# A float32 encoder trunk: VectorE's runs split, and the forget gate turned by VectorE and ScalarE in place of TensorE

## The reference, cut to what matters

```
def swiglu(h, w_in, w_out):
    a, b = jnp.split(h @ w_in, 2, axis=-1)
    return (jax.nn.silu(a) * b) @ w_out

# the recurrence of layer 1
proj = h @ w_in
q, f_pre, v, g_out = jnp.split(proj, 4, axis=-1)
f = lower_bound + (1.0 - lower_bound) * jax.nn.sigmoid(f_pre)
log_f = jnp.log(f); k = 1.0 - f
# per head of 128 features: scores from q, k and the running sum of log_f, then
# o = scores @ v, normalised, times silu(g_out), @ w_out

# the modulation, six vectors a layer, that scale, shift and gate both branches
mod = silu(c) @ w_ada[layer] + b_ada[layer]
```

## Time and profile before

| | us |
|---|---|
| median of 3 runs | 2146.22 (2145.55 to 2146.92) |
| the profiled execution, its own time | 2145.66 |
| its span, first to last instruction | 2143.9 |
| TensorE busy | 2086.6 (97% of the span) |
| VectorE busy | 1573.3 (73%) |
| ScalarE busy | 1142.7 (53%) |
| mean granted clock of TensorE | 0.989 of full speed |

### The profile page before, as it was taken

One profiled execution on the slowest core, in us unless ns is written; L12 is line 12 of the kernel. 1 busy time (PEld: TensorE's weight loads), 2 busy tenths in 40 slices (PEclk: granted clock), 3 DMA queues, 4 the chain that ended last, 5 costly groups with the idle time before them and its releaser, 6 DMA issues.

```text
span 2143.9 us, 25007 instructions
## 1 busy us (share of the span) xinstructions
PE 2086.6 (97%) x9575; PEld 1673.6 (78%) x9575; DVE 1573.3 (73%) x1617; ACT 1142.7 (53%) x1446; POOL 25.6 (1%) x95
## 2 busy tenths in 40 slices
PE   6879999999999999999999999999999999999998
PEld 2437888877788888788888888878888888888886
DVE  1248998889999887789897887677756676557645
ACT  2415544676665443465555565544456877654443
POOL 2000000000000000020000000000000000000000
PEclk7999999999999999999999999999999999999999
DMA  9999987788899898667676664678855666668664
GB/s 398 417 418 377 369 308 266 273 296 281 286 364 352 328 338 299 225 253 246 236 254 210 234 223 149 190 268 312 287 184 183 204 187 200 193 196 299 233 215 146
DMA packets 149594, 573.33 MB, mean 267 GB/s; under 512 B 17169, under 2 KB 17361, under 8 KB 141921
## 3 DMA queue, kind: packets, MB, share of 16 engines
q1 hardware_dynamic: 149474, 571.73, 75.3%
HBM read 569.56 MB, written 2.10 MB: 267 GB/s over the span
## 4 chain that ended last, share of the span: by engine, by line
PE 87%; DVE 5%; DMA 3%; ACT 3%; issue 2%; SPq 0%; DVEq 0%; ACTq 0%
PE prod L694 27%; PE prod L698 27%; PE prod L695 27%; PE modp L735 2%; DVE w_lo L1477 1%; ACT part_value L1264 1%; DMA ada_head<-in_ada_sections 1%; DMA ada_head<-in_ada_mixed 1%; DMA ada<-in_ada_sections 1%; DVE acc L1518 1%; ACT w_hi L1072 1%; PE small L986 1%; PE small L961 0%; PE small L794 0%; PE prod L668 0%
## 5 line engine op out<-in xcount | busy, mean ns | idle before, releaser
L1072 ACT ACTIVATE w_hi<-raw 128x1024 fp32r<-128x1024 f32 x696 | 735.3, 1060 | 791.7 <-PE prod L698 708.0
L1477 DVE TENSOR_TENSOR w_lo<-raw,w_hi 128x1024 fp32r<-128x1024 f32 x696 | 846.9, 1221 | 404.3 <-ACT w_hi L1072 400.7
L694 PE MATMUL prod<-w_hi,h_hi 128*128 128x512 f32 x2072 | 816.6, 394 | 9.0 <-DVE w_lo L1477 7.2
L695 PE MATMUL prod<-w_lo,h_hi 128*128 128x512 f32 x2072 | 807.7, 390 | 0.0
L698 PE MATMUL prod<-w_hi,h_lo 128*128 128x512 f32 x2072 | 807.7, 390 | 0.0
L694 PEld LDWEIGHTS prod<-w_hi,h_hi 128*128 128x128 f32 x2072 | 389.7, 188 | 97.6 <-DVE w_lo L1477 7.8
L698 PEld LDWEIGHTS prod<-w_hi,h_lo 128*128 128x128 f32 x2072 | 389.5, 188 | 82.0 <-DVE h_lo L1630 0.3
L695 PEld LDWEIGHTS prod<-w_lo,h_hi 128*128 128x128 f32 x2072 | 389.7, 188 | 78.7 <-issue 0.5
L1518 DVE SCALAR_TENSOR_TENSOR acc<-ada,cond,acc 128x1024 f32<-128x1024 f32 x255 | 325.8, 1278 | 1.9 <-DMA ada<-in_ada_sections 0.9
L694 PE MATMUL prod<-w_hi,g_hi 128*128 128x512 f32 x680 | 265.6, 391 | 0.0
L698 PE MATMUL prod<-w_hi,g_lo 128*128 128x512 f32 x680 | 264.6, 389 | 0.0
(11 more groups left out here) (217 smaller groups left out, 1030.3 us busy)
## 6 DMA issues: line engine op xcount, KB each, us to landing
raw<-in_w_ffn_in SPq DMA_DIRECT2D x352, 512.0 KB, 4.5
ada<-in_ada_sections SPq DMA_DIRECT2D x256, 512.0 KB, 6.0
raw<-in_w_ffn_out SPq DMA_DIRECT2D x176, 512.0 KB, 4.5
raw<-in_hgrn_w_in SPq DMA_DIRECT2D x128, 512.0 KB, 3.6
ada_head<-in_ada_sections SPq DMA_DIRECT2D x36, 1024.0 KB, 16.4
raw<-in_hgrn_w_out SPq DMA_DIRECT2D x32, 512.0 KB, 3.5
ada<-in_ada_sections SPq DMA_DIRECT2D x12, 1024.0 KB, 18.5
ada<-in_ada_mixed SPq DMA_DIRECT2D x16, 512.0 KB, 8.1
```

The source lines that it names most:

```text
L694: pe.matmul(o, hi[:, k, ts], wh, start=(begin and s == 0), stop=False)
L695: pe.matmul(o, hi[:, k, ts], wl, start=False, stop=False)
L1072: act.activation(w_hi[:, slot], raw[:, r], ACT.Copy).then_inc(hi_ready, 1)
L1477: dve.tensor_tensor(w_lo[:, slot], raw[:, r], w_hi[:, slot], ALU.subtract).then_inc(lo_ready, 1)
```

## The change

It has four parts.

1. **FFN blocks, VectorE** (both layers). The multiplication moves from step 4 to step 5 (`multiply_value`) and the turn from step 4 to step 7, so that one `w_lo` stands between the multiplication and the turn. ScalarE's sixteen copies begin one step later (`MOVE` 2).
2. **The forget values** of the recurrence. TensorE's eight transposes go. At step 22 of VectorE's list it turns the squares of `tok` into `feat` (`turn_forget`), ScalarE places them by sixteen plain copies to `fT` (`move_forget`, two a step from step 25 to 32), and one sigmoid of 128x1024 in place follows at step 34.
3. **Folds.** The unit (1, SC_F, 0) has its folds in steps 14 to 54 of the recurrence (before 16 to 80), (1, G_M, 1) in 62 to 126 (before 92 to 156) and (1, G_F, 0) in 136 to 248 (before 168 to 256).
4. **The bias of gate units** is added to the first row after the sixth fold and to the second after the twelfth (before, to both after the sixteenth), with a wait for each.

The squares of the output norm are kept in `kT` in place of `fT`.

```
-    MOVE, MOVES, HIGH = 1, 2, 2
+    MOVE, MOVES, HIGH = 2, 2, 2
...
+    SQUARES_F, MOVES_F = KD + LD + 1, KD + LD + 4
...
-              ((1, G_M, 0), OUT0 + 120, OUT0 + 166, H0 + 14), ((1, SC_F, 0), H0 + 16, H0 + 80, None),
-              ((1, G_M, 1), H0 + 92, H0 + 156, W0 + 47), ((1, G_F, 0), H0 + 168, H0 + 256, A1 + 14),
+              ((1, G_M, 0), OUT0 + 120, OUT0 + 166, H0 + 14), ((1, SC_F, 0), H0 + 14, H0 + 54, None),
+              ((1, G_M, 1), H0 + 62, H0 + 126, W0 + 47), ((1, G_F, 0), H0 + 136, H0 + 248, A1 + 14),
...
-        sq = fT[:, :, :].rearrange("p a s -> p (a s)").rearrange("p (t n) -> p t n", t=TB)
+        sq = kT[:, :, :].rearrange("p a s -> p (a s)").rearrange("p (t n) -> p t n", t=TB)
...
-                    if at == TURN_F:
-                        evacuated(pe, C_H + 4 * i)
-                        turn_heads(i, "f", lambda tb, b: tok[:, tb, b * P:(b + 1) * P])
...
+            def move_forget(i, n):
+
+                t_at, f_at = n // (P // SQUARE), n % (P // SQUARE)
+                act.wait_ge(forget_turned, i + 1)
+                found = feat[t_at * SQUARE:(t_at + 1) * SQUARE].rearrange("p a b s -> p (a b s)").rearrange(
+                    "p (b k f r) -> p f k b r", b=TB, k=HG, f=P // SQUARE)[:, f_at]
+                into = fT[f_at * SQUARE:(f_at + 1) * SQUARE].rearrange("p k (b t r) -> p t k b r", b=TB, t=P // SQUARE)[:, t_at]
+                act.activation(into, found, ACT.Copy).then_inc(forget_moved, 1)
...
+                    for n in range(2 * (at - MOVES_F), 2 * (at - MOVES_F + 1)):
+                        if 0 <= n < QUADS:
+                            move_forget(i, n)
                     if at == TURN_F + 1 + LA:
-                        heads(fT, i, "f", ACT.Sigmoid)
+                        act.wait_ge(forget_moved, (i + 1) * QUADS)
+                        act.activation(fT[:, :, :], fT[:, :, :], ACT.Sigmoid).then_inc(forget_ready, 1)
...
+                if is_gate(u) and k % 6 == 5:
+                    ada_used(dve, n)
+                    add_bias(u, k // 6)
...
+                def multiply_value(j):
+                    pv = part_value[:, j]
                     dve.wait_ge(silu_ready, layer * NA + j + 1)
                     evacuated(dve, base_b + 2 * j + 1)
                     dve.tensor_tensor(tok[:, :, :], tok[:, :, :], pv, ALU.mult).then_inc(hidden_ready, 1)
...
-                        if j and k == LD - 1:
-                            if j <= NA:
-                                add_value(j - 1)
-                            else:
-                                take_value(base_b, j - 1)
+                        if 0 < j <= NA and k == LD - 1:
+                            add_value(j - 1)
+                        if 0 < j <= NA and k == LD:
+                            multiply_value(j - 1)
+                        if j > NA and k == LD - 1:
+                            take_value(base_b, j - 1)
+                        if j and k == LD + 2:
                             turn_hidden(layer, j - 1)
...
+            def turn_forget(i):
+                evacuated(dve, C_H + 4 * i)
+                dve.wait_ge(forget_moved, i * QUADS)
+                dve.transpose(feat[:, :, :, :].rearrange("p a b s -> p (a b s)"),
+                              tok[:, :, :].rearrange("p a n -> p (a n)")).then_inc(forget_turned, 1)
+
             def forget(i):
-                for half in range(2):
-                    dve.wait_ge(small_free[half], bank_use(half, i, "f"))
+                dve.wait_ge(forget_ready, i + 1)
```

More of the change, by code:

```diff
@@ L277, in bank_use @@
         def bank_use(half, i, what, j=0):
-            order = ["f", "q"] + [("l", k) for k in range(NLV) if k % 2 == half] + ["s"]
+            order = ["q"] + [("l", k) for k in range(NLV) if k % 2 == half] + ["s"]
             if i == NCH - 1:
-                order = ["f", "q"]
+                order = ["q"]
                 steps = [(at, ("l", k)) for k, at in enumerate(LEVEL[i]) if k % 2 == half]
@@ L1979, in in_out @@
                             take_value(C_B[layer], NF - 1)
+                        if n == 0 and k == LD + 2:
                             turn_hidden(layer, NF - 1)
```

22 lines of the change are left out of this document (13 added, 9 removed).

## The result

The changed kernel takes 2169.89 us (median of 4 runs, 2168.09 to 2171.24), the kernel before 2145.89 in the same series: ratio 1.0111, 95% interval 1.0094 to 1.0129. The profiled execution of the changed kernel took 2168.09 us by its own time, the shortest of the four, with a span of 2166.4.

What follows compares the result with a forecast made beforehand. TensorE, busy 97% of the span, was taken as the bound: 2145.66 - 3.5 (transposes) + 10.3 (layer 0) + 3.3 (layer 1) + 6.4 (recurrence) = 2162.2, given as 2162 us. Range 2145 to 2173; the forecast's own 2156 to 2170, chance 0.60.

Steps and rivals of the forecast that it cites:

- The period in the blocks: FFN blocks: turns 22.7 us apart without a fold, 23.7 to 25.1 in layer 0; TensorE loses 10.3 and 3.3 us.
- In layer 0 this loop sets the pace already, not the length of VectorE's run: Layer 0's blocks: turn releases ScalarE, ScalarE releases VectorE, VectorE reaches the next turn; 22.08 us against TensorE's 21.76.
- 4.7 against 5.0: Layer 0's blocks: six periods exceed TensorE's need by 4.7 us, about the 5.0 TensorE waits for `w_lo`.
- The transposes' 3.5 us: Recurrence: dropping TensorE's eight forget transposes wins 0.88 us in each of four groups, 3.5 in all.
- The recurrence: Later `forget` and moved folds cost 3.7, 3.0, 0.3 and -0.6 us by group, 6.4 in all, before 3.5 won.
- `forget` is behind the `w_lo` of that `w_hi`, so it is 2.3 later too: Recurrence groups 1 to 3: forget copies delay ScalarE's `w_hi` of step 34 by 2.3 us, hence VectorE's `forget`.
- the added folds of group 0: Two more folds (2.38 us) ahead of the first level, and later additions: TensorE waits 1.4, 1.2 and 1.1, together 3.7.
- the end of the `pairs` wait: End of recurrence group 3: fewer folds and bias rows remove TensorE's 1.5 us wait and its restart, -1.7.
- A: Faster: VectorE's run length alone makes the block waits, and parting it ends them; 2135.7 us, chance 0.16.
- B: Blocks lose but the recurrence nothing, VectorE's gaps covering added folds, 2156; or layer 0's lower bound, 2155; chance 0.10.
- D: Worse: late `w_lo` frees `raw` slots late, so loads delay ScalarE inside the blocks' loop; 2174 us, chance 0.06.
- E: Recurrence: the forget copies and turn aren't hidden, as the page's transpose rule would have it; 2186 us, chance 0.02.

Runs made afterwards that it cites:

- MOVE = 3 and HIGH = 6: ScalarE's sixteen copies begin behind one more `w_hi`, `g_hi` and `g_lo` move to step 6: 2146.88 us on the kernel before, 2146.39 with only part 1 added.
- the turn two steps earlier: Kernel before with only part 1, but the turn right behind the multiplication (LD, not LD + 2): 2149.89 us, ratio 1.0017.
- The run that was to win the 5 us by a shorter loop: Kernel before with the sixteen copies behind one more `w_hi` and `g_hi`, `g_lo` moved from step 2 to step 6: 2146.88 us, ratio 1.0003.
- the run with short folds: Kernel before with only part 1, MOVE = 3 and HIGH = 6, layer 0's block folds cut to 64 of 1024 columns: 2138.85 us, ratio 0.9966.
- parts 3 and 4 alone: Kernel before with only the new fold spans of three gate units and the bias rows added halfway: 2146.96 us, ratio 1.0003.
- part 1 alone: Kernel before with only the FFN block change (MOVE 2, multiplication a step behind the add, turn at LD + 2): 2161.85 us, ratio 1.0072.
- the copy of q in place: Kernel before with only the forget values' change, and ScalarE's copy of q into `tok` put ahead of Ln: 2146.14 us, ratio 1.0003.

## Why the prediction was right, and where it was not

- **The period in the blocks: right.** Turns of layer 0 from the third to the ninth end at 447.56, 471.36, 496.56, 521.17, 544.96, 568.95 and 594.15: 23.80, 25.20, 24.61, 23.79, 23.99, 25.20, each 0.1 above the forecast; 14.5 from the turn's end to the end of the `w_hi` behind `g_hi` (forecast 14.4). These are VectorE's rows from the fourth turn to the fifth, against the earlier trace rows:

```profile
470.12 1.24 DVE L1886 STREAM_TRANSPOSE feat<-tok 128x1024 f32<-128x1024 f32 x1
...
485.92 1.22 DVE L1493 TENSOR_TENSOR w_lo<-raw,w_hi 128x1024 fp32r<-128x1024 f32 x1 [1.69 <-ACT w_hi L1074]
487.06 1.22 DVE L1892 TENSOR_TENSOR g_lo<-part_value,g_hi 128x1024 fp32r<-128x1024 f32 x1
488.20 1.28 DVE L1534 SCALAR_TENSOR_TENSOR acc<-ada,cond,acc 128x1024 f32<-128x1024 f32 x1
489.39 1.22 DVE L1493 TENSOR_TENSOR w_lo<-raw,w_hi 128x1024 fp32r<-128x1024 f32 x1
490.53 1.22 DVE L1954 TENSOR_TENSOR part_value<-prod,part_value 128x1024 f32<-128x1024 f32 x1
491.85 1.23 DVE L1960 TENSOR_TENSOR tok<-tok,part_value 128x1024 f32<-128x1024 f32 x1
492.99 1.22 DVE L1493 TENSOR_TENSOR w_lo<-raw,w_hi 128x1024 fp32r<-128x1024 f32 x1
494.12 1.28 DVE L1534 SCALAR_TENSOR_TENSOR acc<-ada,cond,acc 128x1024 f32<-128x1024 f32 x1
495.32 1.24 DVE L1886 STREAM_TRANSPOSE feat<-tok 128x1024 f32<-128x1024 f32 x1
```

  The sum of the step can be read off it row by row: `w_lo`, `g_lo`, `w_lo`, add, multiplication, the new `w_lo`, the turn, and two folds between them. Layer 0 cost 10.9 (forecast 10.3), layer 1 4.2 (3.3): turns 22.80 apart (22.7), and TensorE's first wait at 1760.95, in the period that ends with the sixth turn. The runs with MOVE = 3 and HIGH = 6 and with the turn two steps earlier show the cause: with less in the loop the cost goes, wholly or by 12 us.
- **"In layer 0 this loop sets the pace already, not the length of VectorE's run": borne out by the traces, not shown by an experiment.** The prediction's evidence was an agreement of sums, 4.7 against 5.0. The trace of the kernel before has more. Followed back from TensorE's wait at 581.95, at each idle time to what released the engine and else to the instruction before, the chain goes from the ninth turn to the third, six times from VectorE to ScalarE and back, by rows like the earlier trace rows, and never through TensorE or a load. The run that was to win the 5 us by a shorter loop missed because it forecast the loop too short; the run with short folds, which won them, doesn't separate the loop from VectorE's load.
- **The transposes' 3.5 us: right in size, 3.2 measured.** Between the same matmuls around each set of eight TensorE gained 0.80, where the prediction had 0.88. The sum agrees: in the recurrence, the excess of TensorE's waits over the pitch is 4.90, 3.44, 2.15 and 0.46 in groups 0 to 3 (the last after the 1.70 of `pairs` that went), 10.9 in all, and less 3.2 that is 7.7 of the 7.9 measured.
- **The recurrence: mis-sized, 7.9 measured against 6.4 - 3.5 = 2.9.** These are 5.0 of the 8 us; the blocks have 1.5, and the rest is that the median lies 1.8 above the profiled execution, less the 0.6 at the end. Group by group 4.9 (3.7), 3.4 (3.0), 2.15 (0.3), 0.46 (-0.6). In group 0 the three waits for `kdec` are near their forecasts (1.66, 1.08 and 1.30 against 1.4, 1.2 and 1.1), and 0.85 at the q transposes comes on top. The failed step is "`forget` is behind the `w_lo` of that `w_hi`, so it is 2.3 later too": I followed the 2.3 down VectorE's list alone. On ScalarE Ln waits for `forget`, and behind Ln stands the copy of q for which TensorE comes next. The wait at q took in most of what I had put at the first levels of groups 1 and 3, and it also came in group 2, where I had let VectorE's idle time absorb it; idle time behind the waiting instruction absorbs nothing. That the wait is at its full 2.15 in group 2 is due to part 3, which took TensorE's reduction from there.
- **Parts 3 and 4 with part 2: the added folds of group 0 and the end of the `pairs` wait right**, by parts 3 and 4 alone (2.8 us of lateness, and no `pairs` row). Costing parts 2 and 3 together was right as well: apart they come to 2.9, together to 9.7, though part of the difference is TensorE's clock.
- **The rivals.** A fell by part 1 alone. B fell: VectorE's lead didn't cover the folds. D has no sign: with part 1 alone ScalarE's idle time in the blocks ends with the turn (41.6 us) and not with `raw` (9.7), and in the changed kernel likewise (41.2 and 15.9; 420 to 610 us). E: the Trainium skill's rule ("VectorE: DVE Perf Modes", section "Rules for kernel authors") gives 128x128 transposes to TensorE. With the copy of q in place the turn on VectorE and ScalarE comes out at 2146.14 against 2146.10, so here neither side of the rule wins anything: in the profiled execution TensorE's 3.2 us go again in later `kdec` (2.6), in `pairs` (1.2) and at the lower clock behind it (1.5).

## What to carry to other kernels

Where an in-order engine is delayed, follow what stands behind the delayed instruction on every engine that waits for it, also the work that needs nothing of it; and look at what hid there before (here a reduction on TensorE) before it is moved. To tell a loop over several engines from a full engine, take the work that nobody waits for out of the loop and see whether the waits go; if they stay, look in the new trace whether the loop is open at all before the engine is called full, for here it had closed again by another instruction, and an edit that makes the engine's work shorter makes the loop shorter too. Two edits that each use up the same spare time can cost little alone and their full price together.
